# RWKV-7 chunks: gram and chain products placed on four corners of TensorE's array, their PSUM banks shared in two pairs

## The reference

```
def _rwkv7_step(S, inp):
    r, dec, k, v, kk, a = inp
    sa = jnp.einsum('bhvk,bhk->bhv', S, -kk)
    S = S * dec[:, :, None, :] + sa[..., None] * (kk * a)[:, :, None, :] + v[..., None] * k[:, :, None, :]
    y = jnp.einsum('bhvk,bhk->bhv', S, r)
    return S, y
```

## Time and profile before

| | |
|---|---|
| median of 3 runs (lowest, highest) | 2832.9 us (2832.81, 2834.57) |
| the profiled execution, its own time | 2835.1 us |
| span in its profile | 2833.3 us |
| TensorE, VectorE, ScalarE, GpSimd at work | 2656.8, 1512.6, 806.7, 278.1 us |
| mean granted TensorE clock | 0.962 of full speed |
| stage `rwkv_chunks` in the span | 1120.5 to 1429.1 us |

### The profile page before, as it was taken

How to read it: one execution, slowest core, us unless ns; L and a number is a source line. 1 busy time by engine, 2 the same in 40 slices (tenths; PEclk the granted TensorE clock), 3 DMA queues, 4 the chain that set the end, 5 groups by cost and what they waited for, 6 DMA issues and landing times. The chain is left out here.

```text
span 2833.3 us, 45315 instructions
## 1 busy us (share of the span) xinstructions
PE 2656.8 (94%) x18034; PEld 1645.7 (58%) x18034; DVE 1512.6 (53%) x2867; ACT 806.7 (28%) x1791; POOL 278.1 (10%) x321
## 2 busy tenths in 40 slices
PE   8998999999986977888889999999999999999997
PEld 5554566666654323788755666655656665656664
DVE  2116888874324448676669999877843222221101
ACT  2224322125534453111112332012345321144411
POOL 0000111000000000000001222001354430000000
PEclk9999999999997986999989999999999999999998
DMA  5101111231103340000243322343366543522322
GB/s 212 33 13 40 54 70 70 68 95 59 39 32 141 121 137 15 4 26 12 93 131 107 113 104 106 118 147 137 107 208 222 174 146 109 167 105 104 134 82 76
DMA packets 87188, 278.69 MB, mean 98 GB/s; under 512 B 18632, under 2 KB 43048, under 8 KB 74624
## 3 DMA queue, kind: packets, MB, share of 16 engines
q1 hardware_dynamic: 74944, 224.64, 23.3%
q0 software_dynamic: 12032, 51.14, 5.6%
HBM read 242.79 MB, written 32.16 MB: 97 GB/s over the span
## 5 line engine op out<-in xcount | busy, mean ns | idle before, releaser
L2064 PE MATMUL tl_P<-base,tl_WU 128*128 128x368 f32 x2112 | 665.3, 477 | 6.3 <-DVE base L2431 6.3
L2064 PEld LDWEIGHTS tl_P<-base,tl_WU 128*128 128x128 f32 x2112 | 403.8, 192 | 261.0 <-issue 15.9
L407 PE MATMUL dp_PS<-base,dp_W 128*128 128x368 f32 x1440 | 467.4, 478 | 0.0
L407 PEld LDWEIGHTS dp_PS<-base,dp_W 128*128 128x128 f32 x1440 | 269.1, 192 | 154.5 <-issue 6.5
L2080 PE MATMUL tl_P<-base,tl_WD 128*128 128x368 f32 x1056 | 332.1, 473 | 0.0
L2080 PEld LDWEIGHTS tl_P<-base,tl_WD 128*128 128x128 f32 x1056 | 199.0, 190 | 125.2 <-issue 4.1
L148 PE MATMUL pa_PG<-pa_W,base 128*128 128x402 f32 (+1 forms) x576 | 198.7, 505 | 7.6 <-DMA pa_W<-in_w_dsa 7.6
L706 DVE TENSOR_SCALAR_CACHE_REDUCE dp_EQ<-dp_SCORE,dp_trial 128x1024 f32<-128x1024 f32 (+1 forms) x186 | 175.9, 946 | 19.9 <-issue 1.1
L148 PEld LDWEIGHTS pa_PG<-pa_W,base 128*128 128x128 f32 (+1 forms) x576 | 107.0, 187 | 94.3 <-issue 14.2
L2372 DVE MAX8 tl_v<-arena 128x8 f32<-128x4100 f32 x32 | 141.8, 4432 | 3.4 <-issue 1.5
L2375 DVE FIND_INDEX8 tl_i<-tl_v,arena 128x8 uint32<-128x4100 f32 x32 | 141.5, 4423 | 0.0
(11 more groups left out here) (391 smaller groups left out, 3484.5 us busy)
## 6 DMA issues: line engine op xcount, KB each, us to landing
tl_WU<-in_wu SPq DMA_DIRECT2D x66, 1024.0 KB, 4.8
tl_WD<-in_wd SPq DMA_DIRECT2D x48, 704.0 KB, 4.0
dp_W<-in_w_rw SPq DMA_DIRECT2D x15, 1024.0 KB, 4.8
arena<-in_wb SPq DMA_DIRECT2D x24, 512.0 KB, 3.7
arena<-in_wo SPq DMA_DIRECT2D x24, 512.0 KB, 3.6
gates<-dp_PX SPq DMA_DIRECT2D x16, 552.0 KB, 3.0
arena<-gates SPq DMA_DIRECT2D x48, 184.0 KB, 3.7
PM_dram<-dp_PMT SPq DMA_DIRECT2D x14, 552.0 KB, 2.7
```

The source lines that it names most:

```text
L407: last = pe.matmul(bank(f)[:, 0:w], W[:, t // 2 % 2, k, 128 * (t % 2):128 * (t % 2) + 128], xT[:, k, c:c + w], start=k == 0, stop=k == KD - 1)
L2064: last = pe.matmul(out[:, 0:W], WU[:, i % 2, o:o + 128], XN[:, k, :], start=k == 0, stop=k == KD - 1)
```

## The change

The four banks become two pairs. `GB` (half of each of its banks, as `G`) takes all four grams one after the other, `C` takes w, u, y, the state, and in its first bank the sample products and the mean, variance and gate sums. Pairs 0 and 1 go to the first bank of a pair, 2 and 3 to the second. For pairs 2 and 3 the token tiles (RM, RN, MV, BK, Z, W1, U, US) now lie on the partitions of the other head: `home` is head g's own half, `crossed` the other one for pairs 2 and 3. The sets that go from one to the other use four corners; those from crossed to crossed (`chain_w_rest`, `chain_u`) and from home to home (`chain_y`'s state term) use two.

Since a gram overwrites what the one before it left, each waits for its reading (`g_dve`, `g_act`). The waits for y, the sample products and the mean, variance and gate sums of the step before, which stood in `chain_y`, stand in `chain_w` now. `chain_s` waits for `y_read` besides, and the sample products and the mean, variance and gate sums for `s_read`. w and y are cut in two, and as their parts write one place from different rows, the second part waits for the end of the first (`part`), with a level set between. The loops of TensorE and VectorE are put in another order; on ScalarE BK is read ahead of squares and root.

```diff
-        G0, G1, C0, C1 = (sc.enter_context(nc.psum_tensor(f"rc_P{i}", [128, 512], F32)) for i in range(4))
+        GB, C = (sc.enter_context(nc.psum_tensor(f"rc_P{i}", [128, 2, 512], F32)) for i in range(2))
+        G = GB[:, :, 0:4 * CH]
...
-        halves = lambda P: P[:, :].rearrange("p (c n) -> p c n", c=4)
-        half = lambda P: P[:, 0:4 * CH].rearrange("p (c n) -> p c n", c=4)
+        halves = lambda P: P.rearrange("p b (e n) -> p b e n", e=2)
+        half = lambda P: P[:, :, 0:2 * CH].rearrange("p b (e n) -> p b e n", e=2)
...
+        HEAD_OF = [(2 * b + e, b, g) for e in range(2) for b in range(2) for g in range(2)]
+        home = lambda p, g: HEADS[g]
+        crossed = lambda p, g: HEADS[g ^ (p // 2)]
...
-                def each(out, lhsT, rhs, n=CH, at=0, step=CH):
-                    for p in range(4):
-                        for g in HEADS:
-                            o = at + step * p
-                            last = pe.matmul(out[g, o:o + n], lhsT(g, p), rhs(g, p), start=True, stop=True)
+                def each(out, held, to, lhsT, rhs, n=CH, at=0, step=CH, start=True, stop=True, loose=False):
+                    for p, b, g in HEAD_OF:
+                        o = at + step * (p % 2)
+                        last = pe.matmul(out[to(p, g), b, o:o + n], lhsT(held(p, g), p), rhs(held(p, g), p),
+                                         start=start and not (loose and p % 2), stop=stop, skip_group_check=loose)
                     return last
 
-                def corners(s, at, lhsT, rhs, home):
-                    for e in range(2):
-                        for b in range(2):
-                            p = 2 * b + e
-                            for g in range(2):
-                                held, out = HEADS[g], HEADS[g ^ b]
-                                if home:
-                                    held, out = out, held
-                                o = at + CH * e
-                                last = pe.matmul(LV[out, s, b, o:o + CH], lhsT(held, p), rhs(held, p), start=True, stop=True)
-                    return last
+                def corners(s, at, lhsT, rhs, back):
+                    held, to = (home, crossed) if back else (crossed, home)
+                    return each(LV[:, s], held, to, lhsT, rhs, CH, at)
...
                     if n >= 1:
-                        pe.wait_ge(g_dve, 3 * n)
-                    each(G0, of(n, BE), both(n), 128, 0, 128).then_inc(gram, 1)
+                        pe.wait_ge(g_act, n)
+                    each(G, home, crossed, of(n, BE), both(n), 128, 0, 128).then_inc(gram, 1)
 
                 def gram_t(n):
-                    if n >= 1:
-                        pe.wait_ge(g_act, n)
-                    each(G1, of(n, AL), of(n, BE), CH, 0, 128)
-                    each(G1, of(n, VV), eye, CH, CH, 128).then_inc(gram, 1)
+                    pe.wait_ge(g_dve, 3 * n + 1)
+                    each(G, home, crossed, of(n, AL), of(n, BE), CH, 0, 128)
+                    each(G, home, crossed, of(n, VV), eye, CH, CH, 128).then_inc(gram, 1)
 
                 def gram_k(n):
-                    pe.wait_ge(g_dve, 3 * n + 1)
-                    each(G0, of(n, KK), both(n), 128, 0, 128).then_inc(gram, 1)
+                    pe.wait_ge(g_dve, 3 * n + 2)
+                    each(G, home, crossed, of(n, KK), both(n), 128, 0, 128).then_inc(gram, 1)
 
                 def rows_bk(n):
-                    pe.wait_ge(g_dve, 3 * n + 2)
-                    each(G1, of(n, BE), eye, CH, 0, 128)
-                    each(G1, of(n, KK), eye, CH, CH, 128).then_inc(gram, 1)
+                    pe.wait_ge(g_dve, 3 * n + 3)
+                    each(G, home, crossed, of(n, BE), eye, CH, 0, 128)
+                    each(G, home, crossed, of(n, KK), eye, CH, CH, 128).then_inc(gram, 1)
...
+                    if c > SAMPLE:
+                        each(C, home, crossed, of(c, AL), lambda g, p: ST[g, p], stop=False, loose=True).then_inc(part, 1)
+                        return
+                    pe.wait_ge(g_dve, 3 * c + 3)
+                    each(C, crossed, home, lambda g, p: MV[g, m, p, CH:128], lambda g, p: RN[g, i, p, CH:128],
+                         stop=False, loose=True).then_inc(part, 1)
+
+                def chain_w_rest(c):
+                    i, m = c % 3, kept(c)
+                    pe.wait_ge(part, 2 * c + 1)
+                    if c > SAMPLE:
+                        pe.wait_ge(g_dve, 3 * c + 3)
+                        each(C, crossed, crossed, lambda g, p: RN[g, i, p, CH:128], lambda g, p: MV[g, m, p, CH:128],
+                             start=False, loose=True).then_inc(w1_done, 1)
+                        return
+                    pe.wait_ge(ss_in, 16)
+                    over_states(c, AL, True).then_inc(w1_done, 1)
...
+                def chain_u(c):
+                    pe.wait_ge(w1_read, c + 1)
+                    pe.wait_ge(z_ready[c % 2], readied(c) + levels(c) + 1)
+                    each(C, crossed, crossed, lambda g, p: Z2[g, c % 3, p, :], lambda g, p: W1[g, p, :]).then_inc(u_done, 1)
+
+                def chain_y(c):
+                    i, m = c % 3, kept(c)
+                    pe.wait_ge(u_read, c + 1)
+                    if c > SAMPLE:
+                        each(C, home, home, lambda g, p: ST[g, p], of(c, RH), stop=False, loose=True).then_inc(part, 1)
+                        return
+                    each(C, crossed, home, lambda g, p: MV[g, m, p, CH:128], lambda g, p: RN[g, i, p, 0:CH],
+                         stop=False, loose=True)
+                    each(C, crossed, home, lambda g, p: US[g, p, :], lambda g, p: RM[g, i, p, 0:CH],
+                         start=False, stop=False, loose=True).then_inc(part, 1)
+
+                def chain_y_rest(c):
+                    i, m = c % 3, kept(c)
+                    pe.wait_ge(part, 2 * c + 2)
+                    if c == SAMPLE:
+                        over_states(c, RH, True).then_inc(y_done, 1)
+                        return
+                    each(C, crossed, home, lambda g, p: MV[g, m, p, CH:128], lambda g, p: RN[g, i, p, 0:CH],
+                         start=False, stop=False, loose=True)
+                    each(C, crossed, home, lambda g, p: U[g, p, :], lambda g, p: RM[g, i, p, 0:CH],
+                         start=False, loose=True).then_inc(y_done, 1)
...
                 def chain_s(c):
                     i = kept(c)
                     pe.wait_ge(g_act, c + 1)
-                    for p in range(4):
-                        o = slice(CH * p, CH * p + CH)
-                        for g in HEADS:
-                            pe.matmul(C0[g, o], BK[g, i, p, CH:128], MV[g, i, p, CH:128], start=True, stop=False)
-                        for g in HEADS:
-                            last = pe.matmul(C0[g, o], BK[g, i, p, 0:CH], U[g, p, :], start=False, stop=True)
+                    pe.wait_ge(y_read, c + 1)
+                    each(C, crossed, home, lambda g, p: BK[g, i, p, CH:128], lambda g, p: MV[g, i, p, CH:128], stop=False,
+                         loose=True)
+                    last = each(C, crossed, home, lambda g, p: BK[g, i, p, 0:CH], lambda g, p: U[g, p, :], start=False,
+                                loose=True)
...
                 def sample_state(p):
                     pe.wait_ge(g_act, SAMPLE + 1)
                     pe.wait_ge(y_read, p + 1)
+                    if p:
+                        pe.wait_ge(s_read, p)
                     pe.wait_ge(spread, p + 1)
                     for k, x in enumerate((big, big2)):
-                        for g in HEADS:
-                            last = pe.matmul(C1[g, :], BK[g, kept(SAMPLE), p, CH * k:CH * k + CH],
-                                             x[g].rearrange("k b v -> k (b v)"), start=k == 0, stop=k == 1)
+                        for g in range(2):
+                            held = crossed(p, g)
+                            last = pe.matmul(C[HEADS[g], 0, :], BK[held, kept(SAMPLE), p, CH * k:CH * k + CH],
+                                             x[held].rearrange("k b v -> k (b v)"), start=k == 0, stop=k == 1)
...
                         chain_w(c)
                     if ahead:
                         level_q(x, 2)
+                    if chain:
+                        chain_w_rest(c)
                     if new:
                         gram_b(n)
-                        gram_t(n)
                     if chain:
                         chain_u(c)
                     if ahead:
                         level_z(x, 2)
                     if new:
-                        gram_k(n)
-                        level_q(n, 0)
+                        gram_t(n)
                     if chain:
                         chain_y(c)
                     if ahead:
                         level_q(x, 3)
+                    if chain:
+                        chain_y_rest(c)
+                    if new:
+                        gram_k(n)
```

(89 more changed lines are left out.)

77 lines of the change are left out of this document (13 added, 64 removed).

## The result

The changed kernel takes 2859.05 us (median of 4 runs, 2857.24 to 2862.68), the kernel before 2832.86 in the same comparison: a ratio of 1.0097, 95% interval 1.0082 to 1.0112. It is **26 us slower**; the forecast of 2835 and its range to 2851 miss it. The profiled execution took 2857.24 us, its span is 2855.4, against 2833.3 before. The stage's first product comes 2.2 us earlier than in the trace of before, and what lies behind the stage is 1.5 us shorter; so all of the loss arises inside the stage.

The account below looks back on a forecast made before the run. TensorE and VectorE both nearly fill a chunk and wait by turns, with VectorE the new order's spine. Start +2.1, sample chunks +2.0, cycles -5.5, last step +2.0 and +1.4 behind give +2.0: 2835 us, range 2822 to 2851.

Parts of the forecast that it names:

- I charge both orders the same for that.: In a cycle, half-clock stretches (some 1.3 us lost) and unexplained TensorE holds (0.82, 2.52) were charged equally to both orders.
- TensorE's chunk falls from 11.0 to 7.9: Faster gram and chain sets on four corners save TensorE 3.1 us in each chunk.
- Start, +2.1: First two gram-only steps go from 7.5 to 8.0 us each, and the first w's come 1.0 later: 2.1 us lost.
- Sample chunks, +2.0: In the four sample chunks, wide products wait for the state's reading: +0.8 in three, -0.4 in the fourth.
- VectorE waits 1.6: In the sample chunks, VectorE waits 1.6 us for the sample products, where it had waited 0.50.
- Cycles, -5.5: Three cycles of four chunks each get 1.84 us shorter, 5.5 us saved together.
- +2.0 in the last step: Last chunks lack grams to fill in, so new waits before state, variance sums and w cost 2.0 us.
- the layout's gain of 1.8: Operations laid out with their waits give a cycle of 55.7 us in the new order against 57.5 in the old.
- Rest, +1.4: Behind the last step, newly uncovered waits cost 1.4 us.
- The first: Rival: TensorE's extra idle time swallows holds and slow stretches, -11 us, 2824 us; chance 22%.
- The second: Rival: idling TensorE gets more half-clock stretches, decisive from five more; one more in 12 chunks, +16, 2851 us; chance 27%.
- The third: Rival: chain and gram sets keep the old distance, stage 32.6 us longer, 2868 us; chance 4%.

Follow-up runs that it names:

- 5: The changed kernel with each chunk's two 128-wide gram sets issued as two 64-wide sets each, same columns; ratio 1.0128 to the kernel before.
- 6: The kernel before with the same split of its two 128-wide gram sets into 64-wide ones; 2844.16 against 2832.57 us, ratio 1.0042.
- 8: The changed kernel with sample products moved to the gram banks and idle products added for TensorE's clock; 2843.97 us, ratio 1.0039 to the kernel before.
- 9: The changed kernel with SyncE's ten loads for the next stage held back until chunk 16's y is done; ratio 1.0083 to the kernel before.
- 10: The kernel before with idle TensorE products placed where its own half-clock stretches come from; ratio 0.9987 to the kernel before.
- 3: The changed kernel with idle products for TensorE at the start, before sample products and behind gate sums; ratio 1.0051 to the kernel before.
- experiment 1: The changed kernel with three runs of back-to-back products, waiting for nothing, put ahead of the chunks; 64-wide sets took 0.43 to 0.47 us each.
- 2: The changed kernel with each gram and chain set's heads issued in order 0, 1, 2, 3 instead of 0, 2, 1, 3; ratio 1.0108.

## Why the prediction was wrong, point by point

**The step that failed** is the one on disturbances: "I charge both orders the same for that." The holds were 6.7 us of PE's waits and became 24.5, and the half-clock stretches grew with them. I read "TensorE holding with nothing to wait for" as an accident. It was the wait for the next page of instructions. A cycle has 3791 loads and products (x1899 and x1892), 14.8 pages; at one in 3.5 us that is 52 of its 61.1 us however quick the sets are, and where sets stand close together the ones that the change made quicker run into it. "TensorE's chunk falls from 11.0 to 7.9" is true of the array and bought next to nothing; experiments 5 and 6 show that instructions have a price, much the same with and without the change. Of the 25.8 us, the two repairs of 8 take away 16.9; most of the 8.9 left is the last cycle's, where 9 ties 7.1 us to late pages.

**The terms.**
- Start, +2.1: measured +9.0. The waits for the shared bank were laid out at full clock. With four-corner sets TensorE idles longer between the waits and stayed at 1.2 GHz; 6.5 come back with idle products. What remains, 2.5, is near the term.
- Sample chunks, +2.0: measured +9.2. The mechanism (products behind the state's reading) was right, "VectorE waits 1.6" was not: 3.3 on average, since the clock falls in the wait and the wide products then take longer (1.46 for six in the earlier trace rows, 2.40 now). Taking it out gave 7.0 back.
- Cycles, -5.5 with +2.0 in the last step: measured +6.4. With idle products in both, the first two cycles are 59.4 and 59.2 before (10) and 60.5 and 60.4 after (3); where both have the clock at 1.00, in the first cycle of 10 and of 8, it is 59.4 against 59.2. So the layout's gain of 1.8 is not there even then. That the holds take it is my reading; no run has the new layout without them. In the last cycle it is SyncE's loads on top (7.1 us in experiment 9).
- Rest, +1.4: measured +1.2.

**The rivals.** The first did not occur. The second named the right sign and one of the causes, and its 2851 was still 8 us short; its point of decision was right in kind, but it counted one more stretch a chunk in the prompt's chunks, and they came in the start and the sample chunks, which it left out. The third is refuted by the set distances. Instruction supply was in none of them, though the earlier trace rows and the instruction queue's line lay open: I never asked what such a wait ends on. The waits on "issue" are not all of one kind: of the 33 of rc_LV's weight loads before (11.9 us), 3 stand at the place modulo 256.

**What was to show it.** Set distances, VectorE's work and the longer waits for sample sums came as said; TensorE's work is 246 instead of 215, at a lower clock; two of three cycles are over 62 and the granted clock, 0.86, is under the bound of 0.9 that I gave.

## What to carry to other kernels

Count a stage's instructions beside its busy time: where TensorE's small products came to more than one page of 256 in 3.5 us, packing them on more corners saved array time only; 64-wide sets back to back cost as much on four corners as on two, and 128-wide ones did not hold. An engine that gets faster inside a loop bound elsewhere idles more, and here that idle time had a price in TensorE's clock; one shared bank made the idle stretch long enough. And an "issue" wait in the middle of a run of like instructions is a reading to explain, not noise to carry along: hold it against the packets of the instruction queue.

## What was not expected of the hardware

TensorE's instructions come in pages of 256. Back to back in experiment 1, at 5 GB/s, 14 of the 15 steps from page to page are 3.45 to 3.73 us long, one is 4.01; in the changed kernel two are 6.5 and 6.3 us long at 1400 to 1413 us, where SyncE's loads run (102 GB/s in the window). The Trainium skill's page "Runtime: NRT & Kernel Launch", section Instruction fetch mechanics, states that the queue is refilled in blocks of 256 instructions, and that crossing a block's boundary is mostly hidden. The block size agrees with the packets and with the holds at every 256th instruction; that the crossing is hidden does not, for 64-wide products: 1.35 to 1.90 us of hold a block in experiment 1. Further, a set that issues four products on one diagonal and then four on the other is as quick as one that alternates (experiments 1 and 2).
